# One 512-column matmul for both activation parts, and a second half-bank to sum

## The reference, cut to what matters

```python
def swiglu(h, w_in, w_out):
    g, u = split_cols(h @ w_in, (D_FF, D_FF))        # D_FF = 2816
    return (jax.nn.silu(g) * u) @ w_out

x = x + 0.5 * swiglu(rms_norm(x, g[0]), ffn1_w_in[layer], ffn1_w_out[layer])
h = rms_norm(x, g[1])
mixed = even_mixer(h, ...)                            # attention or convolution, in and out projections
x = x + mixed
x = x + memory_cross_attention(rms_norm(x, g[2]), rms_norm(mem, g[3]), ...)
x = x + 0.5 * swiglu(rms_norm(x, g[4]), ffn2_w_in[layer], ffn2_w_out[layer])
```

## Time and profile before

| | |
|---|---|
| median of 3 runs | 2406.56 us (2395.4 to 2407.18) |
| the profiled execution | 2406.13 us, span 2404.3 us |
| TensorE matmul busy | 2291.9 us (95%), 18446 instructions |
| VectorE busy | 1537.7 us (64%) |
| ScalarE busy | 1184.5 us (49%) |
| mean granted TensorE clock | 0.978 of full |

### The profile page before, as it was taken

How to read it: one execution, slowest core, us unless ns; L and a number is a source line. 1 busy time by engine, 2 the same in 40 slices (tenths; PEclk the granted TensorE clock), 3 DMA queues, 4 the chain that set the end, 5 groups by cost and what they waited for, 6 DMA issues and landing times.

```text
span 2404.3 us, 44793 instructions
## 1 busy us (share of the span) xinstructions
PE 2291.9 (95%) x18446; PEld 2197.9 (91%) x18446; DVE 1537.7 (64%) x2216; ACT 1184.5 (49%) x1747; POOL 129.8 (5%) x146
## 2 busy tenths in 40 slices
PE   6999998889999999998999999998999999998998
PEld 6999876879999999787999999986999999998998
DVE  5766647566666765776666666667665666666664
ACT  5644434555446544445554544444544544426543
POOL 2000000110001001000100000100100000001001
PEclk9999987899999999999999999999999999999999
DMA  7556422326555557343455655642655565543653
GB/s 236 190 180 185 149 70 93 106 88 198 184 189 184 189 185 228 106 144 120 141 194 183 196 183 180 219 141 72 192 184 182 180 191 180 162 141 106 194 188 110
DMA packets 383369, 393.27 MB, mean 164 GB/s; under 512 B 6512, under 2 KB 381424, under 8 KB 383040
## 3 DMA queue, kind: packets, MB, share of 16 engines
q1 hardware_dynamic: 381248, 383.30, 49.9%
q0 software_dynamic: 1920, 7.11, 1.0%
HBM read 389.34 MB, written 1.05 MB: 162 GB/s over the span
## 4 chain that ended last, share of the span: by engine, by line
PE 87%; DVE 6%; ACT 4%; issue 1%; POOL 1%; DMA 1%; SPq 0%; POOLq 0%; ACTq 0%; DVEq 0%
PE acc L531 25%; PE acc L535 25%; PE acc L532 24%; PE wide L674 2%; PE acc L549 2%; PE acc L551 2%; PE acc L550 2%; ACT w_hi L815 1%; PE wide L647 1%; DVE w_lo L1048 1%; DVE hn_lo L1080 1%; POOL t L1432 1%; PE wide L663 1%; DMA raw<-in_ffn_w_in 1%; PE wide L602 1%
## 5 line engine op out<-in xcount | busy, mean ns | idle before, releaser
L815 ACT ACTIVATE w_hi<-raw 128x1024 fp32r<-128x1024 f32 (+1 forms) x742 | 768.7, 1040 | 963.8 <-PE acc L535 864.2
L1048 DVE TENSOR_TENSOR w_lo<-raw,w_hi 128x1024 fp32r<-128x1024 f32 (+1 forms) x742 | 889.2, 1201 | 536.1 <-ACT w_hi L815 533.2
L531 PE MATMUL acc<-hn_hi,w_hi 128*128 128x256 f32 x3536 | 855.7, 283 | 37.3 <-DMA colc<-in_cols 18.3
L532 PE MATMUL acc<-hn_lo,w_hi 128*128 128x256 f32 x3536 | 846.2, 280 | 0.0
L531 PEld LDWEIGHTS acc<-hn_hi,w_hi 128*128 128x128 f32 x3536 | 671.2, 190 | 50.7 <-DMA colc<-in_cols 18.3
L532 PEld LDWEIGHTS acc<-hn_lo,w_hi 128*128 128x128 f32 x3536 | 671.5, 190 | 0.5
L535 PE MATMUL acc<-hn_hi,w_lo 128*128 128x256 f32 x3536 | 482.1, 279 | 0.0
L535 PEld LDWEIGHTS acc<-hn_hi,w_lo 128*128 128x128 f32 x3536 | 442.2, 189 | 0.0
L531 PE MATMUL acc<-hid_hi,w_hi 128*128 128x256 f32 x1408 | 334.5, 278 | 0.0
L532 PE MATMUL acc<-hid_lo,w_hi 128*128 128x256 f32 x1408 | 334.5, 278 | 0.0
L532 PEld LDWEIGHTS acc<-hid_lo,w_hi 128*128 128x128 f32 x1408 | 265.3, 188 | 0.0
(11 more groups left out here) (199 smaller groups left out, 2036.4 us busy)
## 6 DMA issues: line engine op xcount, KB each, us to landing
raw<-in_ffn_w_in SPq DMA_DIRECT2D x88, 1024.0 KB, 5.1
raw<-in_ffn_w_out SPq DMA_DIRECT2D x32, 1024.0 KB, 5.2
raw<-in_ffn_pre_w_gate SPq DMA_DIRECT2D x22, 1024.0 KB, 5.3
raw<-in_ffn_pre_w_up SPq DMA_DIRECT2D x22, 1024.0 KB, 5.3
raw<-in_ffn_post_w_gate SPq DMA_DIRECT2D x22, 1024.0 KB, 5.3
raw<-in_ffn_post_w_up SPq DMA_DIRECT2D x22, 1024.0 KB, 5.3
raw<-in_x_w_kv SPq DMA_DIRECT2D x16, 1024.0 KB, 5.4
raw<-in_ffn_pre_w_down SPq DMA_DIRECT2D x16, 1024.0 KB, 5.1
```

Source lines behind the costliest of these rows:

```text
L531: nc.tensor.matmul(bank, wh[:, j, :], a_hi[:, u.k0 + j, :], start=u.first and j == 0, stop=False)
L532: nc.tensor.matmul(bank, wh[:, j, :], a_lo[:, u.k0 + j, :], start=False, stop=False)
L815: nc.scalar.activation(w_hi[:, u.slot, 0:u.nk, :], raw[:, u.raw % RING, 0:u.nk, P * u.half:P * u.half + P], ACT.Copy).then_inc(w_hi_ready, 1)
L1048: nc.vector.tensor_tensor(w_lo[:, u.slot, 0:u.nk, :], raw[:, u.raw % RING, 0:u.nk, P * u.half:P * u.half + P], w_hi[:, u.slot, 0:u.nk, :]. ...
```

## The change

For each block j of a unit of mode F one matmul with `w_hi` now streams the high and the low activations together, 512 columns, into all 512 columns of the bank; right behind it comes the matmul with `w_lo` by the high activations, 256 columns, into the first half. The wait for `w_lo` stands before the first of these. The high and low parts of an activation become one tile. The second half of the bank holds the product with the low activations (`cross`) and has to be added on evacuation: ScalarE copies it to SBUF, VectorE adds it to the first half and then goes on as before. In output projections of the mixers VectorE adds both halves to `x` from PSUM, without a copy.

```diff
+        hn = sb("hn", [P, 2, KB, T], F32R)
+        mn = sb("mn", [P, 2, KB, T], F32R)
+        hn_hi, hn_lo, mn_hi, mn_lo = hn[:, 0], hn[:, 1], mn[:, 0], mn[:, 1]
...
+        cross = sb("cross", [P, BANKS, T])
...
                 if u.mode == "F":
                     wh, wl = w_hi[:, u.slot], w_lo[:, u.slot]
-                    bank = out_ap(u.out)
+                    both, bank = acc[:, u.out % BANKS, :].rearrange("p (s t) -> p s t", s=2), out_ap(u.out)
+                    def low(j):
+                        return nc.tensor.matmul(bank, wl[:, j, :], a[:, 0, u.k0 + j, :], start=False,
+                                                stop=u.last and j == u.nk - 1)
                     for j in range(u.nk):
                         if fresh:
                             pe.wait_ge(r_hi, 8 * u.need + j + 1)
                             pe.wait_ge(r_lo, 8 * u.need + j + 1)
-                        nc.tensor.matmul(bank, wh[:, j, :], a_hi[:, u.k0 + j, :], start=u.first and j == 0, stop=False)
-                        nc.tensor.matmul(bank, wh[:, j, :], a_lo[:, u.k0 + j, :], start=False, stop=False)
-                    pe.wait_ge(w_lo_ready, i + 1)
-                    for j in range(u.nk):
-                        mm = nc.tensor.matmul(bank, wl[:, j, :], a_hi[:, u.k0 + j, :], start=False,
-                                              stop=u.last and j == u.nk - 1)
+                        nc.tensor.matmul(both, wh[:, j, :], a[:, :, u.k0 + j, :], start=u.first and j == 0, stop=False)
+                        if j == 0:
+                            pe.wait_ge(w_lo_ready, i + 1)
+                        mm = low(j)
...
+            def copy_cross(i):
+                act.wait_ge(unit_done, i + 1)
+                o = units[i].out
+                nc.scalar.activation(cross[:, o % BANKS, :], cross_ap(o), ACT.Copy).then_inc(cross_out, 1)
...
                     for h in range(2):
+                        copy_cross(u0 + h)
                         split_after(u0 + h)
                         act.wait_ge(gate_evac, m0 + h + 1)
...
                     for h in range(2):
+                        copy_cross(u0 + 2 + h)
                         split_after(u0 + 2 + h)
                         act.wait_ge(hid_mul, m0 + h + 1)
...
+            def add_cross(out, i, rows=slice(0, P)):
+                dve.wait_ge(unit_done, i + 1)
+                dve.wait_ge(cross_out, crossed[i])
+                o = units[i].out
+                return nc.vector.tensor_tensor(out, out_ap(o)[rows], cross[rows, o % BANKS, :], ALU.add)
...
                     elif u.mode == "F":
-                        ins = nc.vector.tensor_tensor(dest_ap(i), ps, rstd[:, 0, :], ALU.mult)
+                        link(add_cross(dest_ap(i), i))
+                        ins = nc.vector.tensor_tensor(dest_ap(i), dest_ap(i), rstd[:, 0, :], ALU.mult)
...
                         if u.src == "hid":
-                            link(nc.vector.scalar_tensor_tensor(hidf[:, k % 2, :], out_ap(u.out), scale, rstd[:, 0, :],
+                            link(add_cross(hidf[:, k % 2, :], n))
+                            link(nc.vector.scalar_tensor_tensor(hidf[:, k % 2, :], hidf[:, k % 2, :], scale, rstd[:, 0, :],
                                                                 ALU.mult, ALU.mult))
...
-                            nc.vector.tensor_tensor(x[:, k, :], x[:, k, :], out_ap(u.out), ALU.add).then_inc(out_evac, 1)
+                            link(nc.vector.tensor_tensor(x[:, k, :], x[:, k, :], out_ap(u.out), ALU.add))
+                            nc.vector.tensor_tensor(x[:, k, :], x[:, k, :], cross_ap(u.out), ALU.add).then_inc(out_evac, 1)
...
                 def scaled(h):
-                    dve.wait_ge(unit_done, u0 + h + 1)
-                    nc.vector.tensor_tensor(silu_g[:, h, :], out_ap(units[u0 + h].out), rstd[:, 0, :], ALU.mult)\
-                        .then_inc(gate_evac, 1)
+                    link(add_cross(silu_g[:, h, :], u0 + h))
+                    nc.vector.tensor_tensor(silu_g[:, h, :], silu_g[:, h, :], rstd[:, 0, :], ALU.mult).then_inc(gate_evac, 1)
                 def mul(h):
...
+                    link(add_cross(hidf[:, h, :], u0 + 2 + h))
+                    dve.wait_ge(silu_done, m0 + h + 1)
+                    nc.vector.tensor_tensor(hidf[:, h, :], silu_g[:, h, :], hidf[:, h, :], ALU.mult).then_inc(hid_mul, 1)
```

More of the change, by code:

```diff
@@ L2 @@
 from contextlib import ExitStack
+from itertools import accumulate
 import numpy as np
@@ L182, in build @@
         freed.append((kind, count[kind]))
+    name_of = {i: name for name, l in lin.items() for i in range(l.u0, l.u1)}
+    crossed = list(accumulate(u.last and u.mode == "F" and (u.src == "hid" or name_of[i][:3] not in ("mix", "xo0", "xo1"))
+                              for i, u in enumerate(units)))
     last_of_load = {u.raw: i for i, u in enumerate(units)}
@@ L221, in build @@
         pos = sb("pos", [P, T], I32)
-        with nc.sbuf_tensor("hid_hi", [P, HB, T], F32R) as hid_hi, nc.sbuf_tensor("hid_lo", [P, HB, T], F32R) as hid_lo:
-            pass
+        cross = sb("cross", [P, BANKS, T])
+        with nc.sbuf_tensor("hid", [P, 2, HB, T], F32R) as hid:
+            hid_hi, hid_lo = hid[:, 0], hid[:, 1]
         work = sb("work", [P, 2 * HB, T])
@@ L238, in build @@
         gate_evac, out_evac = sem("gate_evac"), sem("out_evac")
+        cross_out = sem("cross_out")
         hn_hi_ready, hn_lo_ready = sem("hn_hi_ready"), sem("hn_lo_ready")
@@ L444, in out_ap, with cross_ap @@
             return acc[:, o % BANKS, 0:T]
+        def cross_ap(o):
+            return acc[:, o % BANKS, T:2 * T]
         def wait_free(eng, o):
@@ L450, in wait_free @@
                 eng.wait_ge((gate_evac, hid_mul, out_evac)[kind], n)
-        name_of = {i: name for name, l in lin.items() for i in range(l.u0, l.u1)}
         def dest_ap(i):
@@ L480, in build @@
         lam_sum, lam_exp, neg_lam = small[:, 40:42], small[:, 42:44], small[:, 44:45]
-        fills = {"hn": (hn_hi, hn_lo, hn_hi_ready, hn_lo_ready), "mn": (mn_hi, mn_lo, mn_hi_ready, mn_lo_ready)}
+        fills = {"hn": (hn, hn_hi_ready, hn_lo_ready), "mn": (mn, mn_hi_ready, mn_lo_ready),
+                 "hid": (hid, hid_hi_ready, hid_lo_ready)}
         def forget_z(i):
@@ L516, in unit @@
                 pe.wait_ge(w_hi_ready, i + 1)
+                a, r_hi, r_lo = fills[u.src]
                 if u.src == "hid":
-                    a_hi, a_lo = hid_hi, hid_lo
                     pe.wait_ge(hid_hi_ready, u.need)
                     pe.wait_ge(hid_lo_ready, u.need)
-                else:
-                    a_hi, a_lo, r_hi, r_lo = fills[u.src]
                 fresh = u.src != "hid" and (i == 0 or (units[i - 1].src, units[i - 1].need) != (u.src, u.need))
@@ L546, in unit @@
                     for j in range(u.nk):
-                        ah, al = a_hi[:, j, P * t:P * t + P], a_lo[:, j, P * t:P * t + P]
+                        ah, al = a[:, 0, j, P * t:P * t + P], a[:, 1, j, P * t:P * t + P]
                         wh, wl = w_hi[:, pair:pair + 2, j, :], w_lo[:, pair:pair + 2, j, :]
@@ L822, in take @@
                         state.evac = freed[units[i].out][1]
+                        if units[i].mode == "F":
+                            copy_cross(i)
                     split_after(i)
@@ L871, in residual @@
                     u = units[n]
+                    if u.last and u.src == "hid":
+                        copy_cross(n)
                     if n < l.u1 - 1:
@@ L1058, in take @@
                     if name == "af":
-                        ins = nc.vector.tensor_tensor(forget_z(0), ps[0:8], rstd[0:8, 0, :], ALU.mult)
+                        link(add_cross(forget_z(0), i, slice(0, 8)))
+                        ins = nc.vector.tensor_tensor(forget_z(0), forget_z(0), rstd[0:8, 0, :], ALU.mult)
                     elif name == "ga":
-                        ins = nc.vector.tensor_tensor(t2[96:128, 6, :], ps[96:128], rstd[96:128, 0, :], ALU.mult)
+                        z = t2[96:128, 6, :]
+                        link(add_cross(z, i, slice(96, 128)))
+                        ins = nc.vector.tensor_tensor(z, z, rstd[96:128, 0, :], ALU.mult)
+                    elif u.mode == "F" and u.src == "mn":
+                        ins = add_cross(dest_ap(i), i)
                     elif u.src == "mn":
@@ L1157, in scaled @@
                 def scaled(h):
-                    dve.wait_ge(unit_done, u0 + h + 1)
-                    nc.vector.tensor_tensor(silu_g[:, h, :], out_ap(units[u0 + h].out), rstd[:, 0, :], ALU.mult)\
-                        .then_inc(gate_evac, 1)
+                    link(add_cross(silu_g[:, h, :], u0 + h))
+                    nc.vector.tensor_tensor(silu_g[:, h, :], silu_g[:, h, :], rstd[:, 0, :], ALU.mult).then_inc(gate_evac, 1)
                 def mul(h):
-                    dve.wait_ge(unit_done, u0 + 2 + h + 1)
-                    dve.wait_ge(silu_done, m0 + h + 1)
                     if m0:
```

(5 more changed lines are left out.)

## The result

The changed kernel takes 2467.97 us (median of 4 runs, 2465.75 to 2470.6) against 2404.52 us before (2395.4 to 2407.18): a ratio of 1.0271, 95% interval 1.024 to 1.0302. That is 63 us slower. The forecast was 2343, the range 2300 to 2400.

What follows compares the result with a forecast made beforehand. The rate of TensorE's matmuls was taken to set the time, then its waits: 2406 us, less 89 from the stream, plus 26 for exposed evacuation, gave 2343 us, range 2300 to 2400.

Steps and rivals of the forecast that it cites:

- the price of the wide matmul: Each block's 512-column matmul: 215.6 ns, its stream covering the load of the low weights; with 116.0 narrow, 331.6 a block.
- the reading of the excess: 256-column float32r matmuls in feed-forward stretches: bound by weight loads, by a few ns; a 512-column one hides the load.
- the 9.3 ns: Time each 256-column matmul costs above its columns: 116.0 ns in feed-forward stretches against 106.7 at 2.4 GHz.
- slower, by the stream: Rival: excess comes from float32r's column each cycle; wide matmul 232 ns, nothing won, 2432 us; decides over 343 ns; chance 0.09.
- The gain term: TensorE's matmul stream: 16.4 ns less a block over 5456 blocks, 89 us saved, bounds 0 to 128.
- The evacuation: Added copies and adds where cover is gone, such as hand-overs, memory norm and start: 26 us, bounds 10 and 55.
- A hand-over behind a projection: Before head norms, rotations and gates: copy 0.45 and add 0.45 us at some 8 places, 7 us.
- The memory norm: Behind it, at two sites, weights and evacuation come late: 5 us a site, bounds 2 and 10, 10 us together.
- Copies: ScalarE's copies of mode F outputs: 522 at 0.40 us, 209 us of ScalarE, beside TensorE.
- the adds: VectorE's adds on evacuation: 554 at 0.42 us, 233 us of VectorE, beside TensorE.
- So 0 in steady stretches: Chunks of four units: low weights keep 4.7 us of cover, so the longer VectorE list costs TensorE 0.
- the two paces of the earlier trace: Feed-forward stretches: 113.3 and near 118 ns a matmul; gain 60 us all quick, 111 all slow; the mixture may shift.

Runs made afterwards that it cites:

- the stream alone: Changed kernel's matmul order with the evacuation of the kernel before, second half of the bank never read: 2440.31 us, ratio 1.0137.
- grouped: Changed kernel with the low pass behind the 8 wide matmuls of a unit instead of between them: 2435.43 us, ratio 1.0116.
- bare stream: Small kernels running only streams of matmuls, computing none of the reference; alternating 512 and 256 float32r columns took 353.4 ns a pair.

## Why the prediction was wrong

**The step that failed is the price of the wide matmul**, "215.6 ns for the wide matmul, the same 512 cycles as the f32 ones", and with it the reading of the excess: "256-column matmuls in float32r are bound by their loads". Most of the 9.3 ns is not a load that ends late. 6.6 of it is the stream, 113.3 ns for 256 float32r columns instead of 106.7, and it doubles at 512, to 226.7. The earlier trace rows did show a pace of loads, 112 ns, just under 113.3; that the two lay close proved nothing, as 113.3 also stands with loads of 64 columns. The earlier trace rows showed 2.2 ns over 512 cycles, but f32, at two cycles a column, does not stand for float32r. The rival "slower, by the stream" said just this, and I gave it 0.09. It priced the wide matmul at 232 ns; 235 was measured, and a pair of 353 where it set the turning point at 343.

The rest of the excess, up to 4.7 ns on 256 columns in the kernel, goes with the loads, but how, the runs leave open: 64-column loads bring 113.3 at 256 columns, but not 226.7 in a stream of 512, and 32-column ones don't bring it when the widths alternate. In the kernel before it came and went by stretches, for a mean of 116.0. In the changed order it was there in every pair: 118 and 235. Hence the stream did not come out at 0, as the rival had it, but at +34.6 us: 5456 pairs at 353.5 against 348.0 are 30 us of it. Why the changed order holds to the slow pace, where three narrow matmuls change between two, is open.

**The gain term**, -89 us, measured +34.6. Its own bounds, 0 to 128, did not hold it: I had let the wide matmul win nothing, but not lose by fixing the slow pace.

**The evacuation**, forecast 26 us, measured 27.7 with the stream held the same. That the two lie so close is luck. The 26 were waits of TensorE over those of the kernel before, and these grew by 7 us only (idle 119.4 against 112.4). Against the stream alone waits make 16 of the 27.7 us, and the clock makes 12, for which the sum had no term. A hand-over behind a projection was priced right, but there are few: TensorE's wait for line 1099 before a rotation is 1.49 us where the wait for line 1065 was 0.5, at two places. The memory norm was priced too dear by more than a factor of three (1.4 a site, not 5). Copies: 522 of 379 ns; the adds 422 ns, both as priced. "So 0 in steady stretches" held.

**The Trainium skill**, "TensorE: Matmul & The Clock Gate", section "Back-to-back issue gap", gives columns over 2.4 GHz plus 2.5 ns as the gap of single matmuls. For bf16 the starts at 215.8 and 109.2 agree with it; for float32r, at 226.7 and 113.3 at best, the measurement decides against it.

**The pace.** I took the two paces of the earlier trace rows as a mixture that might shift. It did, wholly to the slow one, and that is a loss by itself. The earlier trace rows could have warned: the same matmuls with the same loads ran at 113.3 and at 118 ns in different stretches, so the length of a load could not be the whole reason.

No version here beats the kernel before. The order without the new evacuation (grouped, some 2408 by subtraction of the 27.7) would only have equalled it. A low pass in bf16 at the end of each unit might win some 7 ns a block (116.0 less 109.2, an estimate of 37 us from the rates); it was not tried as a whole kernel.

## What to carry to other kernels

Price a matmul from rows of its own type: a wide float32r matmul won nothing over two narrow ones, because the excess over its columns grew with them. Before an edit that merges instructions, run the new sequence as a bare stream, here 512 and 256 alternating, and set it beside the pace of the kernel's own trace: 353.4 against 348.0 ns would have told the sign. Streams of one width alone would not have told it, for they promise a gain (three of 120.0 against 226.7 and 120.0). Price, too, what the longer waits do to the clock: behind five of the seven waits of 1.7 us it fell to half, and behind the 1.4 us at the same places of the kernel before it did not. And where the kernel before shows two paces in like stretches, compare kernels over many runs, and ask which of the two the new order will fix.

## What was not expected of the hardware

A float32r stream takes at best 226.7 ns for 512 columns and 113.3 for 256 at full granted clock, 0.4427 ns a column, and 3 to 5 ns more than that at the widths between; bf16 takes 215.8 and 109.2, its columns and 2.5 ns. Streams of narrow float32r matmuls with 128-column loads hold one of several paces, 113.3 or 118 ns in the kernels and 120 in the bare streams, for whole stretches. Runs of the kernel before differ by over 30 us (2393.86 to 2425.56 in twelve), those of the changed kernel by 5; that the paces are the reason is likely, not shown. VectorE busy in SBUF, or DMAs at 350 GB/s, change none of the rates of 256, 512 and alternating columns.
